# A two-block decoder step on one core: the first PEER query slot goes by token tile, expert rows are mixed inside later slots, eight conditioning slots are summed on VectorE, and the modulation rows are spread in the dilated heads

## The reference

```python
# first block, layer 0: gated linear recurrence; layer 1: stick-breaking attention
h = h + rglru_block(rms_norm(h), ...)          # ... @ a_w_out   ("a_out")
h = h + o @ b_w_o                              # layer 1         ("bo")
# both layers: PEER, 8 heads x 16 experts of 16384 for each token
q = xt @ w_q                                   # 1024 x 2048     ("peer_q", 4 slots)
s = einsum('thpd,hpnd->thpn', q, sub_keys)     # key scores, top 16 of each half, top 16 of 256
act = gelu(einsum('cd,ckd->ck', xc, u_tab[eidx]))
h = h + einsum('ck,ckd->cd', gates * act, v_tab[eidx])
h = h + sigmoid(rms_norm(h) @ w_gate) * (p_i @ w_proj)      # ("ple_gate", 2 slots)
# second block: a conditioning vector makes six rows of 1024
mod = silu(c) @ w_ada + b_ada                  # 1024 x 6144     ("ada", 12 slots)
shift_m, scale_m, gate_m, shift_f, scale_f, gate_f = split(mod, 6)
hm = rms_norm(x, g_pre_mix) * (1 + scale_m) + shift_m
y = hybrid_mixer(hm) @ w_out     # 8 dilated attention heads, 4 recurrent heads ("mix_in", "mix_out")
x = x + gate_m * rms_norm(y, g_post_mix)
hf = rms_norm(x, g_pre_ffn) * (1 + scale_f) + shift_f
x = x + gate_f * rms_norm(moe_ffn(hf), g_post_ffn)          # 32 experts, 4 for each token
```

## Time and profile before

| | us |
|---|---|
| median of 3 runs (lowest, highest) | 2979.68 (2979.44, 2984.55) |
| the profiled execution | 2979.7 |
| its span in the trace | 2977.9 |
| TensorE busy | 2640.7 (89%) |
| VectorE busy | 1325.4 (45%) |
| ScalarE busy | 621.6 (21%) |
| GpSimd busy | 488.7 (16%) |
| HBM traffic | 1049.89 MB, 353 GB/s in the mean |
| mean granted TensorE clock | 0.957 |

### The profile page before, as it was taken

One profiled execution on the slowest core, in us unless ns is written; L12 is line 12 of the kernel. 1 busy time (PEld: TensorE's weight loads), 2 busy tenths in 40 slices (PEclk: granted clock), 3 DMA queues, 4 the chain that ended last, 5 costly groups with the idle time before them and its releaser, 6 DMA issues.

```text
span 2977.9 us, 28431 instructions
## 1 busy us (share of the span) xinstructions
PE 2640.7 (89%) x9642; PEld 1213.3 (41%) x9642; DVE 1325.4 (45%) x3327; ACT 621.6 (21%) x1240; POOL 488.7 (16%) x526
## 2 busy tenths in 40 slices
PE   8987777987899987787988799989999999999998
PEld 7653333333365653333433366543333232333333
DVE  5356777776425457777786432341111111111111
ACT  3122212232125122222232121211111111111111
POOL 0123333343200123333333200000000000000000
PEclk9998999999899999989999999789999999999999
DMA  4499999999753499999999753746999999899997
GB/s 187 152 414 421 421 422 421 421 416 421 316 239 127 163 410 421 422 421 421 421 421 420 309 216 122 274 197 284 422 421 422 422 422 422 353 422 422 384 396 294
DMA packets 145292, 1049.89 MB, mean 353 GB/s; under 512 B 16272, under 2 KB 16528, under 8 KB 17968
## 3 DMA queue, kind: packets, MB, share of 16 engines
q0 software_dynamic: 74064, 537.56, 43.5%
q1 hardware_dynamic: 70560, 509.12, 41.9%
q10 hardware_dynamic: 576, 2.13, 0.2%
HBM read 1047.69 MB, written 1.05 MB: 352 GB/s over the span
## 4 chain that ended last, share of the span: by engine, by line
PE 54%; DMA 37%; DVE 5%; ACT 2%; issue 1%; DVEq 1%; SPq 0%; POOL 0%; POOLq 0%
PE psum L561 13%; DMA uv_more<-in_peer_uv,rows_of 13%; DMA big<-in_moe 13%; DMA big<-in_peer_uv,rows_of 11%; PE psum L918 11%; PE psum L447 9%; PE psum L944 5%; PE psum L462 5%; PE psum L830 1%; PE psum L899 1%; DVE big L1524 1%; PE psum L630 1%; DVE uv_more L1524 1%; PE psum L912 1%; ACT gdiag L1027 1%
## 5 line engine op out<-in xcount | busy, mean ns | idle before, releaser
L561 PE MATMUL psum<-big,gdiag 128*128 128x512 f32 x1880 | 921.9, 647 | 241.3 <-ACT gdiag L1027 241.1
L1524 DVE CUSTOM_DVE_ANT_0 big<-psum,big 128x1024 f32<-128x1024 f32 x470 | 574.4, 1224 | 291.2 <-DMA big<-in_peer_uv,rows_of 285.8
L561 PEld LDWEIGHTS psum<-big,gdiag 128*128 128x128 f32 x1880 | 378.7, 207 | 777.9 <-issue 447.0
L1938 POOL DMA_INDIRECT big<-in_peer_uv,rows_of x470 | 444.1, 945 | 1158.0 <-PE psum L561 764.1
L918 PE MATMUL psum<-big 128*64 128x512 f32 x2240 | 500.7, 596 | 24.1 <-POOLq L1960 23.5
L1904 DVE TENSOR_SCALAR big<-psum 128x512 f32<-128x512 f32 x35 | 24.2, 692 | 665.0 <-PE psum L918 665.0
L918 PEld LDWEIGHTS psum<-big 128*64 128x64 f32 x2240 | 152.8, 137 | 370.3 <-issue 272.5
L447 PE MATMUL psum<-big,ring 128*128 128x256 f32 x1280 | 281.3, 380 | 3.9 <-DVE big L1308 3.7
L447 PEld LDWEIGHTS psum<-big,ring 128*128 128x128 f32 x1280 | 241.7, 190 | 39.4 <-DVE big L1308 4.5
L944 PE MATMUL psum<-ring,big 128*64 128x512 f32 x1120 | 248.1, 594 | 3.8
L1021 ACT ACTIVATE gelu<-dots,rstd 128x4 f32<-128x4 f32 x128 | 38.0, 297 | 885.8 <-DVE dots L1524 885.8
(11 more groups left out here) (376 smaller groups left out, 1848.7 us busy)
## 6 DMA issues: line engine op xcount, KB each, us to landing
big<-in_moe SPq DMA_DIRECT2D x256, 1024.0 KB, 20.4
ring<-in_moe SPq DMA_DIRECT2D x128, 1024.0 KB, 19.0
ring<-in_peer_wq SPq DMA_DIRECT2D x16, 1024.0 KB, 7.2
big<-in_ada SPq DMA_DIRECT2D x16, 1024.0 KB, 14.4
ring<-in_mix_in SPq DMA_DIRECT2D x14, 1024.0 KB, 7.3
ring<-in_a_in SPq DMA_DIRECT2D x8, 1024.0 KB, 7.3
ring<-in_ple_gate SPq DMA_DIRECT2D x8, 1024.0 KB, 8.7
ring<-in_kv SPq DMA_DIRECT2D x8, 1024.0 KB, 7.1
```

The costliest lines, as they stand in the source:

```text
L561: mm = pe.matmul(psum[:, OUT_BANK[t] + c, :], gdiag[:, n % DIAGS, :], uv[(PICKS * l + n) % ROWS][:, D + c * 512:D + (c + 1) * 512], start= ...
L1524: j = dve.tensor_tensor_reduce(out=u, in0=x, in1=u, scale=1.0, scalar=0.0, op0=ALU.mult, op1=ALU.add, accum_out=dots[:, n:n + 1])
L1938: pool.indirect_dma_start(uv[g % ROWS], None, table, bass.IndirectOffsetOnAxis(rows_of[:, n:n + 1], 0)).then_inc(uv_loaded[g % ROWS], 16)
```

## The change

- **First slot by tile.** `first_heads` replaces the common slot code for slot 0 of `peer_q`: features of token tile 0 (32 matmuls of 128 columns), its key scores, then the same for tile 1. `topk` of a pair waits for its own tile's scores.
- **Rows mixed inside later slots.** Rows 0 to 3 are mixed in the middle of slot 2, 4 to 7 after its scores, 8 to 11 in the middle of slot 3; ScalarE's `exponents` and `batch` move to match.
- **Eight conditioning slots on VectorE.** Parts 0 and 2 are loaded beside `a_out` and `bo`. `sums(s)` multiplies each of a slot's eight 128x512 pieces by a column of the conditioning vector and adds them up; three sums stand before the first three adds of the residual, the fourth before the first `topk`. `turn_condition` of these slots stands in `first_heads`. Part 1 stays on TensorE in the first `ple`; the second `ple` and the dilated heads have none. `ada_more` is gone from the ring.
- **mix_in by tile.** Tile 0 of the mixer's input is turned between the halves of the second `ple` gate, and the first `mix_in` slot runs tile 0, then tile 1 (`features_by_tile`).
- **Rows in the dilated heads.** The known row vectors are computed at the start of the mixer, and each dilated head has one `spread`; `mix_out` has none.

```diff
...
-    ("mix_in", 7, ("AA", "DD", "AA", "AA", "AA", "AA", "DD")), ("ada_more", 4, "A"), ("mix_out", 2, "DD"),
+    ("mix_in", 7, ("AA", "DD", "AA", "AA", "AA", "AA", "DD")), ("mix_out", 2, "DD"),
...
+                if l == 0:
+                    sp.wait_ge(v_done, PICKS)
+                    conditioning(1, range(8))
+
+            def conditioning(part, halves):
+                for r in halves:
+                    sp.dma_start(side[part][r], d["ada"][4 * part + r // 2, :, r % 2 * 2048:r % 2 * 2048 + 2048].rearrange(
                         "p (k f) -> p k f", k=4)).then_inc(side_loaded[r // 2], 16)
...
             plain("a_y", d["a_in"][0:2])
+            sp.wait_ge(cond_ready, 1)
+            conditioning(0, range(2))
             plain("a_out", d["a_out"])
+            sp.wait_ge(gated_ready, 1)
+            conditioning(0, range(2, 8))
             peer(0)
...
-            plain("bo", d["bo"])
+            load(FIRST["bo"], d["bo"][0])
+            sp.wait_ge(z_done, 4)
+            conditioning(2, range(2))
+            load(FIRST["bo"] + 1, d["bo"][1])
+            sp.wait_ge(o_done, HEADS // 2)
+            conditioning(2, range(2, 8))
...
-            plain("ada_more", d["ada"][8:12])
...
             def turn_condition(s):
 
-                if s >= 8:
-                    pe.wait_ge(act_took, TILE_NTH[ENDS[FIRST["ada_more"] + s - 8] - 1])
+                if 4 <= s < 8:
+                    pe.wait_ge(cond_took, s - 3)
+                    x = mod_rows[:, s % 2, :]
                 else:
-                    pe.wait_ge(cond_took, s + 1)
+                    pe.wait_ge(sums_ready, s % 4 + s // 8 * 4 + 1)
+                    x = side[s // 4][s % 4 * 2][:, 0, :]
                 for j in range(4):
-                    mm = pe.matmul(psum[:, 3, 4 * s + j:4 * s + j + 1], mod_rows[:, s % 2, j * P:(j + 1) * P], unit[:],
...
+                def first_heads():
+
+                    n = FIRST[f"peer_q{l}"]
+                    w = slot_in(n).rearrange("p (k f) -> p k f", k=KC)
+                    m = ENDS[n] - 4
+                    turn(i, h)
+                    for t in range(TT):
+                        pe.wait_ge(xT_ready, 4 * i + 4 * l + 2 * t + 2)
+                        bank_free(m + 2 * t)
+                        for f in range(4):
+                            for k in range(KC):
+                                mm = pe.matmul(psum[:, (m + 2 * t) % 3, f * P:(f + 1) * P], w[:, k, f * P:(f + 1) * P],
+                                               xT[:, k, t * P:(t + 1) * P], start=(k == 0), stop=(k == KC - 1))
+                        mm.then_inc(tile_done, 1)
+                        for s in range(2 * t, 2 * t + 2):
+                            turn_condition(8 * l + s)
+                        if t == 0:
+                            pe.wait_ge(keys_loaded, 16 * (l + 1))
+                        pe.wait_ge(act_took, TILE_NTH[m + 2 * t])
+                        bank_free(m + 2 * t + 1)
+                        for f in range(4):
+                            mm = pe.matmul(psum[:, (m + 2 * t + 1) % 3, f * P:(f + 1) * P], qT[:, f, t * P:(t + 1) * P],
+                                           keys[:, f * NK:(f + 1) * NK], start=True, stop=True)
+                        mm.then_inc(tile_done, 1)
+
+                first_heads()
+                turn_back(0)
+                def mix_early(at):
+                    for n in range(at, at + BATCH):
+                        mix_rows(n)
+
+                def half_way(at):
+                    return lambda j: mix_early(at) if j == 1 else None
+
+                for s in range(1, 4):
+                    features(f"peer_q{l}", s, xT, between=half_way(8 * s - 16) if s >= 2 else None)
...
-                    if s == 0:
-                        turn_back(0)
                     if s == 2:
-                        for n in range(BATCH):
-                            mix_rows(n)
+                        mix_early(BATCH)
...
-                for n in range(BATCH, PICKS):
+                for n in range(3 * BATCH, PICKS):
...
+                    if l and s == 0:
+                        turn(6, first, (0,), 6)
+                if l:
+                    return
...
+            def features_by_tile(stage):
+
+                n = FIRST[stage]
+                w = slot_in(n).rearrange("p (k f) -> p k f", k=KC)
+                m = ENDS[n] - 2
+                for t in range(TT):
+                    if t:
+                        turn(6, hs, (1,))
+                    pe.wait_ge(xT_ready, 30 + 2 * t)
+                    for g in range(2):
+                        if t == 0:
+                            bank_free(m + g)
+                        for f in range(2):
+                            c = (2 * g + f) * P
+                            for k in range(KC):
+                                mm = pe.matmul(psum[:, (m + g) % 3, f * T + t * P:f * T + (t + 1) * P], w[:, k, c:c + P],
+                                               xT[:, k, t * P:(t + 1) * P], start=(k == 0), stop=(k == KC - 1))
+                        if t:
+                            mm.then_inc(tile_done, 1)
+
+            features_by_tile("mix_in")
+            pe.wait_ge(prod_taken, 4)
...
-                if a % 2 == 0:
-                    condition(8 + a // 2)
-                else:
-                    turn_condition(8 + a // 2)
+                row(a)
...
-            tokens("mix_out", 0, xT, between=lambda j: rows(((0, 1), (2,), (3,), (4,))[j]))
-            tokens("mix_out", 1, xT, between=lambda j: rows(((5, 6), (7,), (), ())[j]))
+            for s in range(2):
+                tokens("mix_out", s, xT)
...
+                for s in range(1, 4):
                     m = tile0(f"peer_q{l}") + 4 * s
                     for g in range(2):
                         act.activation(qT[:, 4 * s + 2 * g:4 * s + 2 * g + 2, :], two(tile_in(m + g)),
                                        ACT.Copy).then_inc(act_took, 1)
+                        if s == 1 and g == 1:
+                            exponents(0)
+                        if s == 2 and g == 0:
+                            batch(0)
+                            batch(4)
+                        if s == 3 and g == 0:
+                            batch(12)
                     for t in range(TT):
                         act.activation(scores[:, t, 4 * s:4 * s + 4, :],
                                        tile_in(m + 2 + t).rearrange("p (a b) -> p a b", a=4), ACT.Copy).then_inc(act_took, 1)
                     if s == 1:
-                        exponents(0)
+                        exponents(1)
                     if s == 2:
-                        exponents(1)
-                        batch(0)
+                        batch(8)
...
+            def sums(s):
+
+                dve.wait_ge(side_loaded[s % 4], 32 * (s // 4 + 1))
+                o = side[s // 4][s % 4 * 2][:, 0, :]
+                for k in range(KC):
+                    w = side[s // 4][s % 4 * 2 + k // 4][:, k % 4, :]
+                    if k == 0:
+                        dve.tensor_scalar(o, w, cond[:, k, 0:1], None, ALU.mult)
+                    else:
+                        i = dve.scalar_tensor_tensor(o, w, cond[:, k, 0:1], o, ALU.mult, ALU.add)
+                    if k < KC - 1:
+                        dve.drain()
+                i.then_inc(sums_ready, 1)
+
+            def add_to_residual(stage, i, part):
                 m = tile0(stage)
                 for g in range(4):
+                    if g < 3:
+                        sums(4 * part + g)
...
+                sums(8 * l + 3)
                 for p in range(2):
                     for _ in topk(p):
                         pass
+                    if p == 0:
+                        modulation(2 * l)
...
+                if l:
+                    gains(6, gm, shift=shift_m, tiles=(0,), banks=6)
```

142 lines of the change are left out of this document (56 added, 86 removed), and 3 rows, old and new, of the table side.

## The result

The changed kernel takes **2955.61 us** (median of 4 runs, 2953.92 to 2960.54) where the kernel before takes 2979.56 beside it: ratio 0.9919, 95% interval 0.9906 to 0.9932. That is 24 us faster. 37.3 were forecast, so the time is 13.6 us above the predicted 2942, inside the range. The profiled execution took 2960.54 (span 2958.7), the longest of the four. One of the 58 executions of changed kernels behind this document took 4413.48 us at a mean granted clock of 0.555 and is left out of all medians.

What follows compares the result with a forecast made beforehand. DMA was taken to bound the two expert gathers and the final MoE, TensorE the stretches between. Savings of 13.2 + 11.5 + 5.7 + 6.9 = 37.3 us from 2979.7 gave 2942 us, range 2930 to 2957.

Steps and rivals of the forecast that it cites:

- Part 1, when the gather starts: PEER start, both layers: first gather 6.9 us earlier, near 131.8; net 6.6 us per layer, 13.2 in all.
- Is TensorE early enough?: PEER slots: TensorE reaches row 12 at about 207, requested bytes take until 206, so the DMA engines do not run dry.
- the prediction's own signs: Gather after PEER start: right if GB/s do not drop between 190 and 210, wrong if they fall in following slots.
- the gather's head start is lost: PEER rival: TensorE reaches row 12 some 6 us late, DMA runs dry, 13.2 shrinks to about 3; 2952 us, chance 0.2.
- Part 2, the sums: Conditioning sums on VectorE beside projections: adds may slip 2 to 3 us, cost nothing overall; bounds 0 to +6.
- Part 3, mix_in: Mixer input's start: tile 0's features under VectorE's normalisation, slot 0 ending 11.5 us earlier; bounds 9 to 12.5.
- Part 4, the heads: Dilated heads 0 to 7: every head takes an odd head's 4.5 us, 31.5 for 37.2, saving 5.7; bounds 0 and 12.
- The heads stay cold: Dilated heads rival: at 1.2 GHz seven heads take 38 us, saving nothing; 2948 us, chance 0.15.
- the sentence on the skill's rule: Dilated heads: by the skill's rule on short bursts, removing long conditioning bursts leaves them cold throughout, 2948 instead of 2942.
- The heads run at their bare work: Dilated heads rival: 3.6 us each, and ScalarE's table load leaves mix_in's start; 2935 us, chance 0.12.
- Part 5, mix_out: mix_out: eight spreads of 0.87 us each are gone, saving 6.9 us; mix_out takes 28 us.
- The low clock in the slots: PEER rival: early-mix waits drop TensorE to 1.2 GHz through slots 2 and 3; +51 us, 3030 us, chance 0.04.

Runs made afterwards that it cites:

- kernel with drains: The changed kernel plus 24 do-nothing drain instructions on ScalarE ahead of its first copy of each PEER block: 2946.34 us, ratio 0.9886.
- second run of the change: The changed kernel run again unedited, on the second chip: 2956.43 us, ratio 0.9922 to the kernel before.
- the second group: Second chip: change unedited 2956.43 us; with 4 drains 2953.34; with 24 drains and mix_in's first slot whole 2960.74, or rows back in mix_out 2969.73.

## Why the prediction was right or wrong

**Part 1, when the gather starts: right.** 131.52 for "near 131.8". The bytes too: in the kernel with drains, with its hand-overs on time, both layers together gain 12.5 us at P, where 13.2 were forecast.

**"Is TensorE early enough?": the step that failed.** It put row 12 at "about 207" and concluded that the DMA engines do not run dry. Undisturbed, row 12 is reached at 206.8 (kernel with drains) and 207.3 (layer 0 of the second run of the change), so the count of features, scores and rows was good; the first profile of the change reaches it at 213.9. What is missing in the sum is a wait: ScalarE takes a tile 4.2 us after TensorE's record of it ends, TensorE stands still for 4.90 us, and the low clock follows. The forecast called it "a near thing" and chose the side without slack; with no slack, a delay of 7 us on TensorE takes all of a layer's 6.6. The transfers measure it: 7.8 us missing in layer 0. By the prediction's own signs this makes it wrong on this point: no drop between 190 and 210 was to be seen, and there are 386 and 395 GB/s, with 312 and 261 on either side.

**Rival "the gather's head start is lost": it came true, from another cause.** It had 0.2 and asked for TensorE 6 us late; it was 6.9 us late (213.9 for 207). It named mixes that wait for rows; those waited 2.99 us, as allowed for. It left 3 of the 13.2 us; -0.9 were left. Its time, 2952, is nearer to the measured 2955.6 than the forecast's.

**Part 2, the sums: right at 0.** The second and third adds of the first projection came 4.8 us later than before (98.38 for 93.58), where 2 to 3 were reckoned, but the fourth at 107.59 for 107.31, and TensorE's PEER start with it.

**Part 3, mix_in: mechanism right, size 7.5 for 11.5.** Slot 1 starts 38.9 us after the gate for a reckoned 34.9. 1.4 us are lost up to tile 1's transposes, as the gate's first half runs partly at the low clock (8.83 for 7.03; 0.81 in 1710:1719), and 2.5 in tile 1's burst, which starts after a wait (granted clock 0.71 in 1739:1749; 9.9 us from its start to slot 1 for 7.4). The prediction's bound of 9 named that burst, and 2.5 is what it allowed; the slow gate it did not have. In the other two profiles of the change the gate takes 7.13 and slot 1 starts 37.2 and 37.1 us after it: 9.3 won, about the bound of 9. So the burst belongs to the change, and the gate's slow start comes in some executions only.

**Part 4, the heads: 8.5 for 5.7.** The forecast took the odd head of before, 4.5 us each; a head with a row takes 3.6 to 3.9 once the clock is up (the last step 2.9) and 5.3 in the first two. These 2.8 us more were not reckoned; they hide half of what parts 3 and 5 fell short. "The heads stay cold" (0.15) and the sentence on the skill's rule would have given 38 us: refuted with rows (28.7), though true of the clock without them. "The heads run at their bare work", 3.6 us each (0.12), did not come: the mean is 4.1 with rows, and without them 4.45.

**Part 5, mix_out: 4.9 for 6.9.** 29.84 for the reckoned 27.8: it starts at the low clock too (0.64 in 1894:1900).

**The low clock in the slots (0.04)** did not come: the change's windows read 0.87 (140:150), 0.79, 0.83, and then 1.00 from 170 to 220.

Parts 3 to 5 give 20.9 for 24.1, PEER -0.9 for 13.2, and 0.8 us are lost in small steps; that is the 19.2 us of span. The median run is 5 us better than the profiled one. On an undisturbed chip the same design with drains gives 32.8 us (2979.17 to 2946.34), 4.5 short of the forecast: in its profile part 1 gives 12.5, part 3 7.4, part 4 9.6, part 5 5.0. So some 9 us (32.8 against 24.0 won, on different chips) go with the lost head start. That the time lies inside the range all the same is due to its upper end of 2957, which has a lost head start in it.

## What to carry over

An earlier start of a transfer stretch is worth something only as far as the engine that frees its buffers keeps up: compare the two times to the first reused buffer, and treat a tie as a likely loss. When a schedule is moved, look at which hand-overs come to lie beside the issue of a long series of gathers, and let the producer have other work before it needs the answer. Compare variants only on one chip, each with the unchanged kernel beside it: here the change reads 2956 us on one chip and 2962 on another (ratios to before 0.9922 and 0.9916), with drains that do nothing 2946 on a third (0.9886), where the unedited change was not run; the second group showed that the drains had no part in it.

## What was not expected of the hardware

- While GpSimd issues a layer's first twelve gathers (g to g+15) and shortly after, ScalarE and SyncE can go on up to 4.5 us after the recorded end of the TensorE tile that they wait for, the last at g+17.1 to g+17.4, in all sixteen layers of eight profiles and in none of the ten of five others. TensorE can stutter in the same stretch (idle 1.50 and 1.02 us without a wait). Its cause stays open. Excluded are a fixed place in ScalarE's program (the lateness moved with the gather, and SyncE shared it) and the table load (the copy ahead of it is late). The Trainium skill, Perfetto Trace Analysis, section Per-instruction lifecycle, says that TensorE's recorded end is an estimate and that the way of a semaphore is not in the profile, and the rows agree that far: they cannot tell a late signal from work that ended later than it is drawn. That GpSimd's issuing is the reason, and not the rows in flight, was not tried.
- Small matmuls put into the waits of a chain shortened it (31.2 to 28.6 us), while the granted clock rose from 0.50 to 0.74.
- The same kernel after the same recorded wait (1.63 us) has run the same 16 records in 8.83 us in one execution and in 7.13 in two others.
